# A hybrid delta-rule and gated-attention block: one table for the inverse norms, gate steps moved into the projections, turned v and k scaled on ScalarE

## The chip, the cores and the metric

The kernel runs on one core of one Trainium2 chip. The metric is the device time of one launch in microseconds; the median of three runs of the kernel before is given below. The engines are named as in the profile: PE (TensorE, matrix products; PEld its weight loads), DVE (VectorE), ACT (ScalarE), POOL (GpSimd), SP (SyncE, which issues the DMAs).

## The reference

The program computes two blocks over 512 tokens of width 1024. The second (three mixers with feed-forward layers) isn't touched by the change. The first is two hybrid layers, each:

```python
proj = x @ w_in                     # dn_q, dn_k, dn_v, dn_z, dn_b, dn_a, g_q, g_k, g_v, g_z, g_r
q, k, v = silu(causal_short_conv([dn_q, dn_k, dn_v], conv_w))     # 4 taps
q, k = l2norm(q) * 128 ** -0.5, l2norm(k)                         # 4 heads of 128
beta = sigmoid(dn_b)
g = -exp(a_log) * softplus(dn_a + dt_bias)
o_dn = head_rms_norm(gated_delta_rule_chunked(q, k, v, g, beta)) * silu(dn_z)
log_f = log_sigmoid(g_r @ gate_w2 + gate_b) / 16
o_gla = head_rms_norm(gla_chunked(g_q / 8, g_k, g_v, log_f)) * silu(g_z)
x = layer_norm(sqrt(2) * x + [o_dn, o_gla] @ w_out)
```

The delta rule works in chunks: with G the running sum of g within a chunk it needs exp(G_i - G_j) under a causal mask, v and k scaled by beta, k scaled by exp(G) and by exp(G_last - G), a triangular solve, and a scan over the chunks' states. The kernel takes chunks of 128 tokens.

## The kernel before, in words

All tiles hold features on the 128 partitions and the 512 tokens along the free axis, in float32; PSUM is eight banks of 128 x 512. A loop runs over the two layers. In each layer the phases follow one another, each a block in which every engine runs its own list of instructions, written out by hand, ordered against the others by semaphores alone; a phase begins when all engines have left the one before. SP clears the semaphores of the phase before at the start of the next.

**hybrid_projections (L321 to L726).** The input weights stream in 14 chunks of 128 x 2048. Each chunk is split into a high part (ACT, `high`, L226) and a low part (DVE, `low`, L237), as is the input (L220, L232), and each product is three matmuls (L251 to L253, or L271 to L273 where the tokens are on the output's partitions). `high(c)` waits for the tiles of chunk c-2 (the buffer is double), `low(c)` for `high(c)`, PE for `low(c)`. Chunks 0 and 1 (q and k of the gated attention) are interleaved by blocks: step n does block n of chunk 0 and block n - `behind` of chunk 1. Before them PE makes small sums (L428: gate rank and logits), which ACT copies (L534); after step 4 PE makes the gate logits from them (L447). ACT then has a chain on these (L539 to L546: bias, Abs, Exp, Ln), DVE goes on with it (L670 to L673: difference and running sum; `apart`, L647 and L648), and then splits chunk 2. ACT, after its chain, takes the first two tiles out, makes `high(2)`, takes the other two, copies `ba` (the beta and decay logits, turned by PE, L453), fills two slots, exponentiates twice (`falls`, L485), and makes `high(3)`. DVE's list for chunk 2 is `low(3)`, then `take(0)`, `take(1)`, ... (L637), which copy score pairs out of the banks. PE issues such a `pair` (L396) after every third block of chunks 2 to 7, and `pair(j)` waits for `take(j-2)`, since pairs use two pairs of banks in turn.

Chunks 8 to 13 are q, k, v of the delta rule: per tile a tap with the last weight on ACT (L505), three more taps on DVE (`conv`, L655), a Silu (L509), and for q and k a square (L515), a sum over the head by a matmul with ones (`sum_squares`, L407, banks 4 to 7 in turn), and the inverse norm `inverse` on ACT: Ln (L521) and then Exp (L524, L527); DVE multiplies it in (`normed`, L660). Inverses 0 to 3 stand in chunk 12's list, 4 to 7 in chunk 13's, two before each tap; `sum_squares(j)` waits for the Ln of `inverse(j-4)`. After chunk 13 come the Silus of the four v tiles.

**delta_gates (L729 to L874).** ACT loads a table that holds both Exp and Ln (`exp_and_log`, L120), and ACT and DVE alternate on tiles of 128 x 16 to make beta and g (L760 to L789). PE sums g (L848), DVE copies it out (L791, `gcol`). POOL spreads g and beta over matrices (L832), PE turns each into a row on all partitions by ones (L855); ACT makes exp of the G row (L771), DVE the differences (L797), `last` (L799), k beta (L801) and k beta exp(G) (L803), ACT the Exp of the differences (L773). POOL makes q exp(G) (L837), the chunk decay (L838) and the causal mask (L842). PE turns v and k (L863) in two banks in turn, and DVE scales them by a column of beta or of exp(G_last - G) as it takes them out (L813). Last, PE makes the products of k with k beta and with q (L872), and DVE multiplies the masked decay in (L821), which waits for all four masks.

**solve, scans, norms_and_output, layer_norm** follow and aren't touched.

Of the kernel before, what the change touches and what calls it, by code (L numbers as in the profile page):

```python
# [320 lines left out]
def hybrid_projections(nc, k, layer, h, gla):  # L321
# [9 lines left out]
    with operands(nc, k, KD), ExitStack() as stack, phase(  # L331
            nc, *GEMM, "parked", "tap", "conv", "silu", "small", "small_out", "logits", "small_turned", "act_step", "log_f",
            "sums", "filled", "slot_filled", "apart", "falls", "scaled", "pair", "taken", "end_arg", "end_exp", "k_end",
            "turned", "turned_read", "square", "square_sum", "inv_ln", "inv_norm", "normed", "z_silu",
            landed=k.landed) as s:
# [3 lines left out]
        small = stack.enter_context(sbuf(nc, "gate_rank_and_logits", [N_SMALL, T], F32))  # L339
        st = Stream(k, k.w_stream, layer * HYBRID_CHUNKS, PROJ_CHUNKS, CHUNK, 2, KD, x,  # L340
# [24 lines left out]
        with nc.Block() as block:  # L365
# [7 lines left out]
            def _(pe):  # L373
# [57 lines left out]
                behind = 2  # L431
                for step in range(KD + behind):
# [11 lines left out]
                    if step == 4:  # L444
# [37 lines left out]
            def _(act):  # L482
# [49 lines left out]
                st.input_high(act, s, 2, 5)  # L532
                act.wait_ge(s.small, 1)
# [24 lines left out]
                falls(1)  # L558
                st.high(act, s, 3, 1)
# [25 lines left out]
                for c in range(8, PROJ_CHUNKS):  # L585
# [33 lines left out]
            def _(dve):  # L619
# [57 lines left out]
                st.low(dve, s, 2, 0)  # L677
                for c in range(2, 8):
# [17 lines left out]
                for c in range(8, PROJ_CHUNKS):  # L696
# [10 lines left out]
                    conv(tile + 1)  # L707
                    if c == 12:
# [20 lines left out]
def delta_gates(nc, k, h, a):  # L729
# [5 lines left out]
    with ExitStack() as stack, phase(  # L735
            nc, "gate_act", "gate_dve", "g_ready", "gcol_sum",
            "gcol", "spread", "row", "row_exp", "diff", "row_read", "decay", "masked", "kb", "scaled", "turned", "turned_read",
# [3 lines left out]
        gt = sb("gate_steps", [P, 8, 16])  # L741
        beta = sb("beta", [P, TT, HEADS])
        g = sb("log_decay", [P, TT, HEADS])
        gcol = sb("g_column", [P, TT, HEADS])
# [5 lines left out]
        ba = h.ba[:].rearrange("p (t c) -> p t c", t=TT)  # L750

        def b16(n):
            return gt[:, n].rearrange("p (t h) -> p t h", t=TT)

        with nc.Block() as block:
            @block.scalar
            def _(act):
                exp_and_log(act)

# [1715 lines left out]
```

## Time and profile before

| | us |
|---|---|
| median of 3 runs (2411.50 to 2412.14) | 2411.68 |
| the profiled execution, its own time | 2410.51 |
| span of its trace | 2408.4 |
| mean granted clock of PE | 0.944 |
| one hybrid layer | 426.6 |

The profile is of one execution. The page gives busy time per engine over the whole span; a window gives it for a stretch, with the granted clock of PE (1.00 is 2.4 GHz, 0.50 is 1.2 GHz). A timeline row is start, duration, engine, line and operation; in brackets stands how long the engine had been idle and whose work ended that. Rows with x2 or more merge neighbours of one line. Durations of neighbours on one engine overlap a little, so start to start is less than their sum.

### The profile page before, as it was taken

Reading aid. Unit: us, or ns where it says so; the run is one execution under the profiler, and the core shown is the slowest. Engines: PE = TensorE matmul, PEld = TensorE weight load, DVE = VectorE, ACT = ScalarE, POOL = GpSimd, SP = SyncE. Lnnn points to the kernel's source line nnn. Section 1 sums busy time; section 2 is a strip of 40 time slices with the busy share of each in tenths; the row PEclk is TensorE's granted clock in tenths of the full one; section 3 lists DMA queues with packets and bytes.
Section 4 is the critical chain, followed back from the end, with each engine's and each line's share of the span. In section 5 each row is a group of like instructions: output and inputs, shape, how many; then the busy total and the mean of one; then the engine's idle time right before and its main releaser. Section 6 shows DMA issues by size and latency. Waiting matters only on the chain. (4 is left out here: it accounts for less than half of the span.)

```text
span 2408.4 us, 28383 instructions
## 1 busy us (share of the span) xinstructions
PE 2106.0 (87%) x11432; PEld 1626.7 (68%) x11432; DVE 1164.2 (48%) x1427; ACT 914.7 (38%) x1257; POOL 346.2 (14%) x332
## 2 busy tenths in 40 slices
PE   7996788799769959988889999979997868999996
PEld 4775586477548638734667788757886746778875
DVE  4444645444464551244367547533113756754753
ACT  4237333624732342255344224323222624432431
POOL 1200623020063300033210000020000022000002
PEclk9998799899979979999999999999999979999998
DMA  5111002221100212100112232212222001223221
GB/s 198 70 70 53 2 18 89 80 79 70 53 1 2 105 37 103 70 1 1 70 70 88 73 112 92 86 59 93 99 88 70 1 35 70 86 74 112 88 90 59
DMA packets 27158, 163.53 MB, mean 68 GB/s; under 512 B 2755, under 2 KB 6267, under 8 KB 11420
## 3 DMA queue, kind: packets, MB, share of 16 engines
q1 hardware_dynamic: 27036, 161.81, 18.9%
q8 instruction: 88, 1.44, 0.2%
q14 instruction: 34, 0.28, 0.0%
HBM read 155.47 MB, written 6.33 MB: 67 GB/s over the span
## 5 line engine op out<-in xcount | busy, mean ns | idle before, releaser
L251 PE MATMUL psum<-inputs_high,weights_high 128*128 128x512 f32 x928 | 376.5, 406 | 5.1 <-DVE inputs_low L232 5.1
L253 PE MATMUL psum<-inputs_high,weights_low 128*128 128x512 f32 x928 | 363.8, 392 | 0.0
L252 PE MATMUL psum<-inputs_low,weights_high 128*128 128x512 f32 x928 | 363.8, 392 | 0.0
L237 DVE TENSOR_TENSOR weights_low<-weights_raw,weights_high 128x2048 fp32r<-128x2048 f32 x72 | 169.4, 2353 | 324.7 <-ACT weights_high L226 324.7
L1771 PE MATMUL psum<-inputs_high,weights_high 128*128 128x512 f32 x704 | 278.8, 396 | 19.9 <-DVE weights_low L1763 11.1
L1772 PE MATMUL psum<-inputs_low,weights_high 128*128 128x512 f32 x704 | 275.7, 392 | 0.0
L1773 PE MATMUL psum<-inputs_high,weights_low 128*128 128x512 f32 x704 | 275.5, 391 | 0.0
L251 PEld LDWEIGHTS psum<-inputs_high,weights_high 128*128 128x128 f32 x928 | 175.6, 189 | 57.4 <-DVE inputs_low L232 7.9
L252 PEld LDWEIGHTS psum<-inputs_low,weights_high 128*128 128x128 f32 x928 | 175.6, 189 | 38.5 <-issue 3.8
L253 PEld LDWEIGHTS psum<-inputs_high,weights_low 128*128 128x128 f32 x928 | 175.5, 189 | 37.5
L1756 ACT CAST weights_high<-weights_raw 128x2048 fp32r<-128x2048 f32 (+1 forms) x76 | 126.7, 1669 | 178.1 <-PE psum L1773 174.8
L1771 PEld LDWEIGHTS psum<-inputs_high,weights_high 128*128 128x128 f32 x704 | 133.2, 189 | 56.1 <-DVE inputs_low L1903 16.4
L226 ACT CAST weights_high<-weights_raw 128x2048 fp32r<-128x2048 f32 x72 | 136.6, 1897 | 88.4 <-PE psum L253 37.5
L1763 DVE TENSOR_TENSOR weights_low<-weights_raw,weights_high 128x2048 fp32r<-128x2048 f32 (+1 forms) x76 | 152.5, 2006 | 36.1 <-ACT weights_high L1756 36.1
L1773 PEld LDWEIGHTS psum<-inputs_high,weights_low 128*128 128x128 f32 x704 | 133.2, 189 | 28.1
L1772 PEld LDWEIGHTS psum<-inputs_low,weights_high 128*128 128x128 f32 x704 | 133.3, 189 | 27.6 <-issue 0.5
L1771 PE MATMUL psum<-hidden_high,weights_high 128*128 128x512 f32 x352 | 140.2, 398 | 10.6 <-DVE weights_low L1763 10.1
L1929 DVE SCALAR_TENSOR_TENSOR conv<-up_scaled,second_parameters,conv 128x511 f32<-128x511 f32 (+1 forms) x176 | 131.9, 750 | 21.6 <-ACT conv L1859 18.5
L1772 PE MATMUL psum<-hidden_low,weights_high 128*128 128x512 f32 x352 | 139.7, 397 | 0.0
L1773 PE MATMUL psum<-hidden_high,weights_low 128*128 128x512 f32 x352 | 139.5, 396 | 0.0
L1922 DVE TENSOR_TENSOR up_scaled<-psum,inverse_rms 128x512 f32<-128x512 f32 x88 | 60.8, 691 | 109.9 <-PE psum L1773 105.8
L1859 ACT ACTIVATE conv<-up_scaled,second_parameters 128x512 f32<-128x512 f32 x88 | 71.9, 817 | 109.4 <-DVE up_scaled L1922 109.4
(317 smaller groups left out, 3360.8 us busy)
## 6 DMA issues: line engine op xcount, KB each, us to landing
weights_raw<-w_stream SPq DMA_DIRECT2D x116, 1024.0 KB, 4.8
weights_raw<-w_down SPq DMA_DIRECT2D x32, 704.0 KB, 4.1
residual_parked<-residual SPq DMA_DIRECT2D x2, 2048.0 KB, 11.1
residual_back<-residual_parked SPq DMA_DIRECT2D x2, 2048.0 KB, 7.9
residual<-x_t SPq DMA_DIRECT2D x1, 2048.0 KB, 7.9
out_t<-residual SPq DMA_DIRECT2D x8, 256.0 KB, 2.0
constants<-consts SPq DMA_DIRECT2D x1, 1537.5 KB, 11.7
table_backward<-bias_rows SPq DMA_DIRECT2D x1, 1024.0 KB, 5.5
```

Of the source, the lines that this page charges most:

```text
L226: act.copy(self.whi[:, u, 0:self.cols], self.raw[:, u, 0:self.cols]).then_inc(s.high, 1)
L237: dve.tensor_tensor(self.wlo[:, u, 0:self.cols], self.raw[:, u, 0:self.cols], self.whi[:, u, 0:self.cols].bitcast(F32), ALU.subtract).then ...
L251: pe.matmul(out, hi, self.ahi[:, k], start=start and b == 0, stop=False)
L252: pe.matmul(out, hi, self.alo[:, k], start=False, stop=False)
L253: mm = pe.matmul(out, lo, self.ahi[:, k], start=False, stop=stop and b == blocks - 1)
L1756: act.copy(whi[:, c % 2, 0:cols], raw[:, c % 2, 0:cols]).then_inc(s.high, 1)
L1763: dve.tensor_tensor(wlo[:, c % 2, 0:cols], raw[:, c % 2, 0:cols], whi[:, c % 2, 0:cols].bitcast(F32), ALU.subtract).then_inc(s.split, 1)
L1771: pe.matmul(out, wh, hi, start=start, stop=False)
L1772: pe.matmul(out, wh, lo, start=False, stop=False)
L1773: return pe.matmul(out, wl, hi, start=False, stop=stop)
L1859: act.activation(y[:, n % 2, yy], up[:, n % 2, yy], ACT.Identity, scale=taps[:, layer, 2, yy, n:n + 1], bias=bias[:, layer, yy, n:n + 1]). ...
L1929: dve.scalar_tensor_tensor(y[:, n % 2, yy, back:], up[:, n % 2, yy, 0:T - back], taps[:, layer, 2 - back, yy, n:n + 1], y[:, n % 2, yy, ba ...
```

## The change

The gate steps (L760 to L789) move from `delta_gates` into `hybrid_projections`: on ACT behind `falls(1)` and ahead of `high(3)`, on DVE behind `low(2)` and ahead of `low(3)`. The G sum (L848) moves to block 8 of chunk 9 on PE, its copy (L791) behind chunk 9's convolutions on DVE, and `sum_squares(0)` waits for it (the G sum lies in bank 6, which the sums of squares use in their turn). The table with Exp and Ln is loaded on ACT ahead of L534 and again ahead of `inverse(0)`. The gate logits L447 go from after step 4 to after step 0, and `behind` from 2 to 3. In `delta_gates` ACT in place of DVE scales the turned v and k, as four activations of 128 x 128 with a column as scale, placed between its Exps; PE's order mixes the turning with rows and products.

```diff
@@ hybrid_projections: phase gains gate_act, gate_dve, g_ready, gcol_sum, gcol; tile gate_steps [P, 8, 16]; b16, ba moved here
@@ tensor
                     elif j == 0:
                         pe.wait_ge(s.taken, n_pairs)
                         pe.wait_ge(s.turned_read, 2)
+                        pe.wait_ge(s.gcol, 1)
...
+                    elif c == 9 and b == 8:
+                        pe.wait_ge(s.g_ready, 1)
+                        pe.matmul(ps[:, 6, 0:16], con[:, K_INCL:K_INCL + P], h.g[:].rearrange("p t h -> p (t h)"),
+                                  start=True, stop=True).then_inc(s.gcol_sum, 1)
...
-                behind = 2
+                behind = 3
...
-                    if step == 4:
+                    if step == 0:
                         pe.wait_ge(s.small_out, 1)
@@ scalar
                 st.input_high(act, s, 2, 5)
+                exp_and_log(act)
                 act.wait_ge(s.small, 1)
...
                 falls(1)
+                act.wait_ge(s.small_out, 2)
+                act.activation(b16(0), ba[:, :, 0:HEADS], ACT.Exp, scale=-1.0).then_inc(s.gate_act, 1)
+                act.activation(gt[:, 7, 0:HEADS], par[:, C_ALOG:C_ALOG + HEADS], ACT.Exp).then_inc(s.gate_act, 1)
+                act.wait_ge(s.gate_dve, 1)
+                act.activation(b16(2), b16(1), ACT.Abs).then_inc(s.gate_act, 1)
+                act.wait_ge(s.gate_act, 3)
+                act.activation(b16(3), b16(2), ACT.Exp, scale=-1.0).then_inc(s.gate_act, 1)
+                act.wait_ge(s.gate_act, 4)
+                act.activation(b16(4), b16(3), ACT.Ln, bias=con[:, K_ONE:K_ONE + 1]).then_inc(s.gate_act, 1)
                 st.high(act, s, 3, 1)
...
                     elif c == 12:
+                        exp_and_log(act)
                         for j in range(4):
                             inverse(j)
@@ vector
                 st.low(dve, s, 2, 0)
+                dve.wait_ge(s.small_out, 2)
...
+                dve.tensor_tensor(b16(1), ba[:, :, HEADS:], dtb, ALU.add).then_inc(s.gate_dve, 1)
...
+                dve.scalar_tensor_tensor(h.g[:], b16(6), -1.0, rate, ALU.mult, ALU.mult).then_inc(s.g_ready, 1)
                 for c in range(2, 8):
...
                     conv(tile + 1)
+                    if c == 9:
+                        dve.wait_ge(s.gcol_sum, 1)
+                        dve.tensor_copy(h.gcol[:], ps[:, 6, 0:16].rearrange("p (t h) -> p t h", t=TT)).then_inc(s.gcol, 1)
@@ delta_gates: the gate steps, gcol and the waits for them go; beta, g, gcol come from h
@@ scalar
+                def turned(n):
+                    hd = n % HEADS
+                    act.wait_ge(s.turned, n + 1)
+                    for t in range(TT):
+                        col = beta[:, t, hd:hd + 1] if n < HEADS else last[:, 1, hd, t:t + 1]
+                        dst = a.vb if n < HEADS else a.kdec
+                        ins = act.activation(dst[:, t, hd], ps[:, 6 + n % 2, t * P:(t + 1) * P], ACT.Copy, scale=col)
+                    ins.then_inc(s.turned_read, 1)
                 exp_and_log(act)
...
                     act.activation(erow[:, n], ps[:, (2 * n) % 4], ACT.Exp).then_inc(s.row_exp, 1)
+                    if n >= 1:
+                        turned(n - 1)
                     act.wait_ge(s.diff, 4 * n + 4)
                     act.activation(decay[:, :, n], decay[:, :, n], ACT.Exp).then_inc(s.decay, 1)
                 act.wait_ge(s.last_arg, HEADS)
                 act.activation(last[:, 1], last[:, 0], ACT.Exp).then_inc(s.last_exp, 1)
+                turned(HEADS - 1)
+                act.wait_ge(s.last_exp, 1)
+                for n in range(HEADS, 2 * HEADS):
+                    turned(n)
@@ vector: the loop of eight multiplications (L805 to L814) goes
@@ tensor: row(n) and turn(n) are L851 to L856 and L859 to L865 as functions
+                for n in range(4):
+                    row(n)
+                turn(0)
+                turn(1)
+                for n in range(4, 2 * HEADS, 2):
+                    row(n)
+                    row(n + 1)
+                    turn(n // 2)
+                for n in range(HEADS, HEADS + 2):
+                    turn(n)
                 pe.wait_ge(s.kb, HEADS)
                 for n in range(2 * TT):
...
                     mm.then_inc(s.pair, 1)
+                    if n in (1, 3):
+                        turn(HEADS + 2 + n // 2)
```

## Rows read from the trace of the kernel before

**Rows 1.** The page of the profiled execution: span, and busy time of TensorE.
```profile
span 2408.4 us, 28383 instructions
...
PE 2106.0 (87%) x11432; PEld 1626.7 (68%) x11432; DVE 1164.2 (48%) x1427; ACT 914.7 (38%) x1257; POOL 346.2 (14%) x332
```

**Rows 2.** One line's instructions: the last gate step, once in each layer.
```profile
L789 DVE SCALAR_TENSOR_TENSOR log_decay<-gate_steps x2: 174/174/174, 246.6 to 673.2; 128x16 f32<-128x16 f32 x2
```

**Rows 3.** Windows of layer 0: length; busy us (instructions) PE, PEld, DVE, ACT, POOL; PEclk, DMA, GB/s.
```profile
24.40:49.10 24.70, 24.63 (x105) 18.85 (x104) 8.12 (x11) 11.93 (x15) 0.00 (x0) 1.00 0.29 120
...
52.10:57.70 5.60, 5.59 (x18) 4.04 (x19) 1.21 (x1) 4.34 (x4) 3.90 (x3) 0.50 0.49 187
...
276.40:328.00 51.60, 44.25 (x1138) 42.24 (x1139) 26.34 (x56) 15.64 (x26) 31.52 (x24) 0.90 0.01 3
```

**Rows 4.** Timeline, start of layer 0: start, us, engine, line, op [idle <-releaser].
```profile
24.60 0.58 ACT L534 COPY gate_rank_and_logits<-psum 40x512 f32<-40x512 f32 x1 [2.42 <-PE psum L428]
...
37.69 1.26 ACT L539 ACTIVATE k_end<-psum,layer_parameters 128x512 f32<-128x512 f32 x2 [10.94 <-PE psum L447]
...
45.14 1.90 ACT L226 CAST weights_high<-weights_raw 128x2048 fp32r<-128x2048 f32 x1
...
52.11 0.79 PE L271 MATMUL psum<-weights_high,inputs_high 128*128 128x512 f32 x1 [3.07 <-DVE weights_low L237]
...
54.57 1.88 ACT L226 CAST weights_high<-weights_raw 128x2048 fp32r<-128x2048 f32 x1
...
58.84 0.76 DVE L637 COPY_PREDICATED gla_scores<-constants,psum 128x512 f32<-128x512 int32 x1
...
62.73 0.49 PE L396 MATMUL psum<-gla_qk 64*128 64x128 f32 x4
```

**Rows 5.** Last projection chunk of layer 0: one group of lines, then the timeline.
```profile
L521 ACT ACT_TABLE_LOAD x8 | 10.3, 1283 | 0.1
...
208.53 0.69 ACT L521 ACTIVATE inverse_norm<-psum,constants 128x512 f32<-128x512 f32 x1
...
212.56 0.69 ACT L521 ACTIVATE inverse_norm<-psum,constants 128x512 f32<-128x512 f32 x1
...
221.47 1.10 PE L407 MATMUL psum<-squares,constants 128*128 128x512 f32 x2 [0.87 <-ACT inverse_norm L521]
...
224.25 0.40 PE L253 MATMUL psum<-inputs_high,weights_low 128*128 128x512 f32 x1
...
239.60 0.67 ACT L505 ACTIVATE conv<-psum,layer_parameters 128x512 f32<-128x512 f32 x1
...
241.59 2.19 ACT L509 ACTIVATE qkv<-conv 128x512 f32<-128x512 f32 x4
```

**Rows 6.** Timeline of the delta gates of layer 0.
```profile
244.05 1.28 ACT L120 ACT_TABLE_LOAD   x1 [0.27 <-PEq L365]
...
246.04 0.31 ACT L767 ACTIVATE gate_steps<-gate_steps,constants 128x16 f32<-128x16 f32 x1
...
246.82 0.61 PE L848 MATMUL psum<-log_decay,constants 128*128 128x16 f32 x2 [22.17 <-DVE log_decay L789]
246.91 1.05 POOL L832 TENSOR_TENSOR spread<-constants,log_decay 128x512 f32<-128x512 f32 x1 [120.62 <-DVE log_decay L789]
...
266.25 0.64 POOL L842 TENSOR_SCALAR_AFFINE_SELECT decay<-decay 128x512 f32<-128x512 f32 x1
...
268.98 0.69 DVE L821 TENSOR_TENSOR a_transposed<-psum,decay 128x512 f32<-128x512 f32 x1 [0.20 <-PE psum L872]
...
275.70 0.69 DVE L821 TENSOR_TENSOR attention<-psum,decay 128x512 f32<-128x512 f32 x1 [0.20 <-PE psum L872]
```

**Rows 7.** Timeline: TensorE's first product of the solve, layer 0.
```profile
278.11 0.68 PE L933 MATMUL psum<-constants,coupling 64*64 64x64 f32 x16 [2.46 <-POOL coupling L1010]
```

**Rows 8.** Groups of lines by form: the turned copies, and a 128x128 activation.
```profile
L813 DVE TENSOR_TENSOR v_beta<-psum,beta 128x512 f32<-128x512 f32 x4 | 2.7, 684 | 0.8 <-PE psum L863 0.8
...
L2183 ACT ACTIVATE scores<-scores,negative_maxima 128x128 f32<-128x128 f32 x72 | 27.8, 388 | 30.8 <-DVE negative_maxima L2159 30.8
```

More of the change, by code:

```diff
@@ L339, in hybrid_projections, with b16 @@
         small = stack.enter_context(sbuf(nc, "gate_rank_and_logits", [N_SMALL, T], F32))
+        gt = stack.enter_context(sbuf(nc, "gate_steps", [P, 8, 16], F32))
+        ba = h.ba[:].rearrange("p (t c) -> p t c", t=TT)
+        def b16(n):
+            return gt[:, n].rearrange("p (t h) -> p t h", t=TT)
         st = Stream(k, k.w_stream, layer * HYBRID_CHUNKS, PROJ_CHUNKS, CHUNK, 2, KD, x,
@@ L735, in delta_gates @@
     with ExitStack() as stack, phase(
-            nc, "gate_act", "gate_dve", "g_ready", "gcol_sum",
-            "gcol", "spread", "row", "row_exp", "diff", "row_read", "decay", "masked", "kb", "scaled", "turned", "turned_read",
+            nc, "spread", "row", "row_exp", "diff", "row_read", "decay", "masked", "kb", "scaled", "turned", "turned_read",
             "last_arg", "last_exp", "pair", "pair_read") as s:
@@ L740, in sb @@
             return stack.enter_context(sbuf(nc, name, shape, F32))
[L741 to L744, printed above, removed]
+        beta, g, gcol = h.beta, h.g, h.gcol
         spread = sb("spread", [P, 2, TT, P])
@@ L757, in _ @@
             def _(act):
-                exp_and_log(act)
-                act.activation(b16(0), ba[:, :, 0:HEADS], ACT.Exp, scale=-1.0).then_inc(s.gate_act, 1)
-                act.activation(gt[:, 7, 0:HEADS], par[:, C_ALOG:C_ALOG + HEADS], ACT.Exp).then_inc(s.gate_act, 1)
-                act.wait_ge(s.gate_dve, 1)
-                act.activation(b16(2), b16(1), ACT.Abs).then_inc(s.gate_act, 1)
-                act.wait_ge(s.gate_act, 3)
-                act.activation(b16(3), b16(2), ACT.Exp, scale=-1.0).then_inc(s.gate_act, 1)
-                act.wait_ge(s.gate_act, 4)
-                act.activation(b16(4), b16(3), ACT.Ln, bias=con[:, K_ONE:K_ONE + 1]).then_inc(s.gate_act, 1)
+                def turned(n):
[6 more added lines that the diff above has]
+                    ins.then_inc(s.turned_read, 1)
+                exp_and_log(act)
                 for n in range(HEADS):
@@ L803, in _ @@
                     dve.tensor_tensor(a.kbg[:, n], kb[:, n], erow[:, n], ALU.mult).then_inc(s.scaled, 1)
-                for n in range(2 * HEADS):
-                    hd = n % HEADS
-                    dve.wait_ge(s.turned, n + 1)
-                    if n == HEADS:
-                        dve.wait_ge(s.last_exp, 1)
-                    src = ps[:, 6 + n % 2].rearrange("p (t e) -> p t e", t=TT)
-                    col = beta[:, :, hd] if n < HEADS else last[:, 1, hd]
-                    dst = a.vb if n < HEADS else a.kdec
-                    dve.tensor_tensor(dst[:, :, hd], src, col.unsqueeze(2).to_broadcast([P, TT, P]),
-                                      ALU.mult).then_inc(s.turned_read, 1)
                 for n in range(2 * TT):
@@ L846, in _, with row @@
             def _(pe):
-                pe.wait_ge(s.g_ready, 1)
-                pe.matmul(ps[:, 6, 0:16], incl, g[:].rearrange("p t h -> p (t h)"), start=True, stop=True) \
-                    .then_inc(s.gcol_sum, 1)
-                for n in range(2 * HEADS):
+                def row(n):
                     pe.wait_ge(s.spread, n + 1)
@@ L856, in _, with turn @@
                               start=True, stop=True).then_inc(s.row, 1)
-                pe.wait_ge(s.gcol, 1)
-                for n in range(2 * HEADS):
+                def turn(n):
                     src = v if n < HEADS else kk
```

35 lines of the change are left out of this document (13 added, 22 removed).

## The prediction

> **What bounds the kernel now.** I read the page first: TensorE (PE) is busy 87% of a span of 2408.4 us [rows 1]. That is an average, so I read the windows of layer 0 next, with the granted clock beside them, then the timeline around the holes. Everything that the change touches lies in the two hybrid layers; the same steps stand 426.6 us later in layer 1 [rows 2], so each term below is worked out for layer 0 and taken twice.
>
> Three holes matter. **The start:** PE is full from 24.4 to 49.1, then stands still for 3.07 us until VectorE (DVE) has split chunk 2, and works on at half clock (1.2 GHz) until about 57.7 [rows 3, 4]. DVE was late because its chain (log of the gate, scan, `apart`) hangs on ScalarE's L539, which waited 10.94 us for PE's logits and began at 37.69 only. **The end of the projections:** PE ends its last product at 224.65, but ScalarE (ACT) works on until 243.78, on eight inverse norms of which each is two table loads of 1.28 us around an Ln and an Exp [rows 5]. PE itself waits there too, for a bank that a late Ln frees (the row shows 0.87; there are three of 0.84 to 0.87). **The delta gates:** from 244.05, GpSimd (POOL) can't begin until 246.91, because the small gate steps come first; its work then runs to 266.89, DVE's products with the mask run from 268.98 to 276.39 [rows 6].
>
> **Part 1, the start.** The preload of the common table (1.28) falls where ACT waits 2.42 us for L428's sums [rows 4]: free. The logits are issued after step 0 instead of step 4. Two steps of 6 and three of 12 products come before them now, so 42 products come off their front; at 24.63 us for some 100 products [rows 3] that is about 10 us. ACT's chain then ends near 33 and DVE is through with `apart` near 39, so the split of chunk 2 hangs on its high half alone, which began at 45.14 and ended at 47.04. With `behind` 3 chunk 0 has 6 fewer products of chunk 1 before its end, 1.4 us: high half at 45.7. From the end of a high half to the end of its split the rows show 2.4 (56.45 to 58.84) [rows 4]: ready at 48.1, before PE ends chunk 1 at 49.0. So the stall of 3.07 and the half clock behind it (5.6 us at half speed, 2.8 lost) go.
>
> What is late next: `pair(2)`, which may not start before DVE's `take(0)`, queued behind the split of chunk 3. ACT loses the load before its Exps (1.28) and gets the gate steps, whose five activations took 245.33 to 246.35, 1.0 us with their handovers [rows 6]. L226 thus starts at 54.3 for 54.57, `take(0)` ends near 59.35, and `pair(2)` starts at 59.4. PE would be there at 62.73 - 3.07 - 2.8 = 56.9, so it waits 2.5. **Gain: 62.73 - 59.4 = 3.3 us.** Queued behind ACT's new waits is only that high half; DVE's new steps fill its wait for it. Bounds: 5.9 if the new wait doesn't exist; 0 if the clock falls again behind it and costs as much as the one that goes. Here the trace warns: behind a hole of 2.46 us (PE at 278.11) the stage ran at 0.90 of the clock [rows 3, 7]. I take 3.3: PE is full on both sides of the new hole, while the thin gate stage lay before the one of 2.46. The Trainium skill (TensorE: Matmul & The Clock Gate, "Why this matters for your kernels") sets its limit at gaps of more than some 3 us. By it the clock stays and 3.3 stands; by the row of the 2.46 us hole it may fall and this part be worth 0. The range keeps both.
>
> **Part 2, chunk 9.** The G matmul (L848, 0.61 us at half clock for its two passes [rows 6]) now stands in a stretch where PE is full: **cost 0.3**. Its copy is done by DVE after two convolutions and holds up `sum_squares(0)` if late; it is small and due in chunk 10, so I count nothing; if that cover were gone it costs under 1 us.
>
> **Part 3, one table.** The 16 loads per layer (8 of them stand in the L521 group, 8 at L524 and L527) become one preload. Ln to Ln was 212.56 - 208.53 = 4.03; less two loads it is 1.46 [rows 5]. That loads aren't put back is shown by the gate steps: Exp, Exp, Abs, Exp, Ln behind one L120 load, none between [rows 6]. ACT needs 1.28 + 8 x 1.46 + a tap of 0.7 from 207.2, so 220.9 if never waiting; the last inverse waits for its sum of squares, at 221.47 - 2.6 + 1.1 = 220.0, and ends at 221.5. PE loses its waits, 2.57, and ends at 222.1: it is the later, so PE sets the end. Behind it the chain is the one of before: tap(11) at 239.60 to the end of the last Silu at 243.78, 4.18 us (it hides the Silu load, the convolution runs beside). New end 222.1 + 4.2 = 226.3. **Gain 17.5 us.** Bounds: 15 if PE keeps its waits, 18 if the Silus overlap better.
>
> **Part 4, the delta gates.** POOL starts at once: 246.91 - 244.1 = 2.8 us. Its twelve steps per head took 19.98 us to the end of the last mask at 266.89 [rows 6] and are untouched, but the row matmuls now have transposes between them: I put 0.6 on it. DVE loses its eight multiplications (0.69 each, 5.5 us [rows 8]) that stood between its head loop and its products, so it no longer comes 22.07 us after POOL's start (268.98) but waits for the mask: 20.6. The eight products took 7.4; with the last two transposes of k among PE's products I give them 7.8. Sum 28.4 for 29.48: 1.1 us. **Gain 3.9 us.** This needs ACT to keep up. Its new operation, 128x128 with a column scale, isn't in the trace; the nearest row is the 128x128 Exp with a column bias, 388 ns [rows 8], so 32 are 12.4 us at most, and with eight Exps of 0.6 to 0.7 that is below 18 in a stage where 20.6 pass before DVE needs anything: hidden, though each head's mask Exp may now come up to 1.5 us later, which POOL's queue covers. Bounds: 0 (the interleaving and a slow clock eat all) and 6 (clock at full, spreads no longer waiting for half-speed rows). No DMA is added, and SP's clears of five semaphores only change phase.
>
> **Sum.** 3.3 - 0.3 + 17.5 + 3.9 = 24.4 a layer, 48.8 for both. The profiled execution took 2410.51 (span 2408.4): 2361.7. The median of the runs is 1.2 higher: **2362.9 us**.
>
> **Rivals.** *A, the delta stage gives nothing (still faster).* If ACT's scaled copies or the shuffled PE queue make masks late, part 4 is 0: 41 us gained, 2371. For it: each head now has one more ACT step in its loop of about 2.6 us. Chance 0.12. *B, the loads come back.* If the compiler reloads per function after a preload of another phase, 16 loads stay and one joins (1.3), and the gate steps add two loads ahead of chunk 3's high half, 2.6 us more wait at `pair(2)`: part 1 is about -2.5 with the clock down, part 3 -1.3, part 4 +3.9: 0, 2412. Against it: the Ln at L767 had none [rows 6]. Chance 0.03. *C, slower: ACT becomes the bound of the delta stage.* The 32 copies run in PE's and DVE's way: PE may not turn the next tile before ACT has read the last but one. ACT is covered up to 20.6 us with about 5 taken, so up to 0.49 us a copy; beyond, each 0.1 us costs 3.2 a layer. To undo the 24.4 takes 32x = 15.6 + 24.4, x = 1.25 us; at 1.4 us the run is 2 x 4.8 slower, 2421. The nearest row is 0.388. Chance 0.02. The Trainium skill (ScalarE: Activation LUTs, "Rules for kernel authors") speaks for C in kind: multiplications belong on VectorE, ScalarE being slower at them. The trace agrees as to size (0.69 for 512 columns on DVE against four of up to 0.39 on ACT), yet DVE was in the way and ACT idle for most of the stage, so the row of the path, not of the engine, decides.
>
> **How the numbers follow.** The forecast has 0.83, A 0.12, B 0.03, C 0.02. Slowest end of the range: part 1 at 0, part 3 at 15.5, part 4 at 0: 15.2 a layer, 2381. Fastest: 5.9, 18 and 5.5: 29 a layer, 2353. Only B and C and a little else lie outside. A measurement of this kernel tells 0.2% (4.8 us) from no change. Faster 0.95, same 0.03, slower 0.02.
>
> **What would show it.** Part 1: chunk 2 starts at 49.1 with no wait, a wait of about 2.5 for `gla_scores` stands before the third pair, and the granted clock says whether it was dear. Part 3: no load between 209 and 223, PE without waits in chunk 13, ACT's last Silu at about 4.2 after PE's end. Part 4: POOL's first spread within 0.4 us of the phase's start, DVE idle ahead of its first product until POOL's last mask, eight groups of four copies of under 0.4 us on ACT. The prediction is wrong if the tail behind PE's last product is longer than 6 us, or if chunk 2 still waits for its split.

## The result, and the profile after

The changed kernel takes 2370.91 us (median of 4 runs, 2369.7 to 2372.03) against 2411.59 of the kernel before, run beside it: a ratio of 0.9834 (95% interval 0.9817 to 0.9851). That is 40.7 us gained where 48.8 were forecast; it lies inside the range. Its profiled execution took 2370.67.

The page of the kernel after, as [rows 1] before:

```profile
span 2368.9 us, 28397 instructions
...
PE 2104.9 (89%) x11432; PEld 1630.0 (69%) x11432; DVE 1157.6 (49%) x1411; ACT 888.5 (38%) x1289; POOL 343.4 (14%) x332
```

PE is as long busy as before (2106.0) and waits some 38 us less. Of the stages, measured in each trace between the same events (in us, layer 0 and layer 1):

| stage, from and to | before | after | gained, both | forecast |
|---|---|---|---|---|
| start: first small product to the last pair's end | 132.49, 132.70 | 132.69, 131.35 | 1.15 | 6.6 |
| on to tap 9 (holds the G matmul) | 59.12, 59.12 | 59.32, 59.36 | -0.4 | -0.6 |
| tail: tap 9 to the last Silu's end | 37.25, 37.25 | 19.06, 19.06 | 36.4 | 35.0 |
| delta gates: to the last product with the mask | 32.62, 32.72 | 28.59, 28.24 | 8.5 | 7.8 |
| solve, scans, norms, out product | 137.88, 137.97 | 139.52, 139.51 | -3.2 | 0 |
| layer norm | 22.14, 22.07 | 22.88, 24.44 | -3.1 | 0 |
| loop back: its end to layer 1's first product | 4.91 | 6.77 | -1.9 | 0 |
| second block and end | 1545.32 | 1543.37 | 1.95 | 0 |

These and 0.2 ahead of the first product make the 39.6 us between the spans. Parts 2 to 4 came within 1.4 us of their forecasts. Two things did not come as forecast: the start, and stages whose code is the same. Each column is one trace, and one code varies from trace to trace: the start of both layers is 265.2 us here before and 263.2 in e1 below, which has the same code there, and 263.1 to 264.8 in five traces with the changed start (after, e2, e5, e8, e10). So the 1.15 us of the start aren't clear of that spread; the 36.4 and the 8.5 are.

**The start** of the kernel after, timeline of layer 0, against [rows 4]: first PE, then POOL, then DVE, each engine's rows by themselves.

```profile
47.82 0.50 PE L271 MATMUL psum<-weights_high,inputs_high 128*128 128x512 f32 x1
...
60.11 1.22 PE L402 MATMUL psum<-gla_qk 64*128 64x128 f32 x8 [4.05 <-DVE gla_scores L659]
...
51.25 1.52 POOL L758 TENSOR_TENSOR qkv<-gla_qk,qkv 128x512 f32<-128x512 f32 x1 [50.73 <-ACT qkv L496]
52.73 1.51 POOL L760 TENSOR_TENSOR qkv<-gla_qk,qkv 128x512 f32<-128x512 f32 x1
54.20 1.53 POOL L758 TENSOR_TENSOR qkv<-gla_qk,qkv 128x512 f32<-128x512 f32 x1
55.70 1.49 POOL L760 TENSOR_TENSOR qkv<-gla_qk,qkv 128x512 f32<-128x512 f32 x1
...
52.26 0.55 DVE L704 TENSOR_SCALAR gate_steps<-gate_steps 128x16 f32<-128x16 f32 x1 [3.79 <-ACT gate_steps L572]
52.84 0.25 DVE L706 RECIPROCAL beta<-gate_steps 128x16 f32<-128x16 f32 x1
53.05 1.23 DVE L708 SCALAR_TENSOR_TENSOR gate_steps<-gate_steps 128x16 f32<-128x16 f32 x1
54.31 1.46 DVE L711 SCALAR_TENSOR_TENSOR log_decay<-gate_steps 128x16 f32<-128x16 f32 x1
55.70 3.64 DVE L237 TENSOR_TENSOR weights_low<-weights_raw,weights_high 128x2048 fp32r<-128x2048 f32 x1
59.26 1.31 DVE L659 COPY_PREDICATED gla_scores<-constants,psum 128x512 f32<-128x512 int32 x2
```

Chunk 2 starts without a wait, at 47.82. But the third pair waits 4.05 us. The last gate step took 0.174 us in the delta stage [rows 2] and takes 1.46 here. Look at the ends: L704 at 52.81, L708 at 54.28, L711 at 55.77, each within 0.05 us of the end of one of POOL's products (52.77, 54.24, 55.73); and the split L237, 3.64 us long, is what is left of POOL's fourth product (to 57.19) plus 2.15, about its usual 2.29. The reciprocal isn't held up. The number of operands doesn't explain that, since L704, which like it reads one tile (and a constant), is held up. In layer 1 the four gate rows have the same lengths, but the split goes ahead of POOL's fourth product instead of behind it, by 0.01 us, and the wait is 2.77:

```profile
464.94 2.28 DVE L237 TENSOR_TENSOR weights_low<-weights_raw,weights_high 128x2048 fp32r<-128x2048 f32 x1
...
464.95 3.63 POOL L760 TENSOR_TENSOR qkv<-gla_qk,qkv 128x512 f32<-128x512 f32 x1
```

The windows around layer 0's wait, with [rows 3] as their counterpart:

```profile
47.80:56.00 8.20, 8.20 (x45) 5.88 (x43) 3.85 (x6) 6.94 (x12) 4.75 (x4) 1.00 0.33 128
56.00:60.10 4.10, 0.07 (x1) 0.02 (x1) 4.10 (x3) 0.00 (x0) 1.19 (x1) 0.88 0.00 0
60.10:65.90 5.80, 5.79 (x21) 4.25 (x23) 1.20 (x2) 0.00 (x0) 0.00 (x0) 0.50 0.50 181
```

PE was full up to the hole and came back at 1.2 GHz for about 5.8 us, which costs 2.9. In layer 1 the half clock behind the wait of 2.77 lasts 3.4 us and costs 1.7. The length isn't fixed by the hole: behind the same hole of 3.07 us PE ran at half clock for 5.6 and 5.8 us in the two layers of the kernel before and for 3.4 in e1's layer 0, whose start is 2.2 us shorter, 1.1 of it by this.

**The tail**, timeline of ACT, against [rows 5]:

```profile
207.42 1.28 ACT L120 ACT_TABLE_LOAD   x1
208.71 0.69 ACT L532 ACTIVATE inverse_norm<-psum,constants 128x512 f32<-128x512 f32 x1
209.43 0.72 ACT L535 ACTIVATE inverse_norm<-inverse_norm,constants 128x512 f32<-128x512 f32 x1
210.06 0.67 ACT L532 ACTIVATE inverse_norm<-psum,constants 128x512 f32<-128x512 f32 x1
...
220.23 0.63 ACT L538 ACTIVATE inverse_norm<-inverse_norm 128x512 f32<-128x512 f32 x1
221.59 0.69 ACT L516 ACTIVATE conv<-psum,layer_parameters 128x512 f32<-128x512 f32 x1 [0.73 <-PE psum L253]
222.29 1.28 ACT L520 ACT_TABLE_LOAD   x1
223.59 2.19 ACT L520 ACTIVATE qkv<-conv 128x512 f32<-128x512 f32 x4
```

One load stands ahead of eight inverses, Ln to Ln is 1.35 where it was 4.03, and the last Silu ends 4.2 us after PE's last product.

**The delta gates**, timeline, against [rows 6]: POOL's first and last row, DVE's products, ACT's and PE's rows on the turned tiles.

```profile
226.06 1.05 POOL L840 TENSOR_TENSOR spread<-constants,log_decay 128x512 f32<-128x512 f32 x1 [99.78 <-POOLq L371]
...
245.95 0.62 POOL L850 TENSOR_SCALAR_AFFINE_SELECT decay<-decay 128x512 f32<-128x512 f32 x1
...
246.68 1.29 DVE L831 TENSOR_TENSOR a_transposed<-psum,decay 128x512 f32<-128x512 f32 x2 [4.64 <-POOL decay L850]
...
234.30 1.14 ACT L794 ACTIVATE v_beta<-psum,beta 128x128 f32<-128x128 f32 x4 [1.02 <-PE psum L868]
...
242.24 2.18 ACT L794 ACTIVATE k_decayed<-psum,to_last 128x128 f32<-128x128 f32 x8
...
242.41 0.66 PE L868 MATMUL psum<-constants,qkv 128*128 128x128 f32 x4 [1.92 <-ACT v_beta L794]
```

POOL starts 0.29 us after the Silus; DVE now idles 4.64 us until POOL's last mask. A group of four scaled copies takes 1.14 us.

### The profile page after: what moved, and what is told of

It is laid out like the page before. It is cut to its first block and busy times, and to the rows that moved or that the text cites. A ratio compares the mean times of both kernels' runs of the same rounds, so it can differ in the third digit from the quotient of the medians.

```text
span 2368.9 us, 28397 instructions
## 1 busy us (share of the span) xinstructions
PE 2104.9 (89%) x11432; PEld 1630.0 (69%) x11432; DVE 1157.6 (49%) x1411; ACT 888.5 (38%) x1289; POOL 343.4 (14%) x332
## 5 line engine op out<-in xcount | busy, mean ns | idle before, releaser
L237 DVE TENSOR_TENSOR weights_low<-weights_raw,weights_high 128x2048 fp32r<-128x2048 f32 x72 | 170.4, 2366 | 328.4 <-ACT weights_high L226 328.4
L1789 PE MATMUL psum<-hidden_high,weights_high 128*128 128x512 f32 x352 | 140.4, 399 | 10.6 <-DVE weights_low L1781 10.2
```

The lines of the kernel that those rows point to most:

```text
L237: dve.tensor_tensor(self.wlo[:, u, 0:self.cols], self.raw[:, u, 0:self.cols], self.whi[:, u, 0:self.cols].bitcast(F32), ALU.subtract).then ...
L1789: pe.matmul(out, wh, hi, start=start, stop=False)
```

## The experiments

Twelve kernels ran in three lots of four, each lot on one chip beside the kernel before; ratios are compared, since the lots' medians of before differ (2413.6, 2414.71, 2413.27). "After" in an edit means the changed kernel.

| kernel | us | ratio, 95% interval |
|---|---|---|
| e1_table_only | 2380.22 | 0.9860, 0.9844 to 0.9877 |
| e2_no_table | 2407.92 | 0.9980, 0.9970 to 0.9989 |
| e3_high_first | 2363.79 | 0.9794, 0.9777 to 0.9810 |
| e4_gates_behind | 2363.53 | 0.9800, 0.9783 to 0.9817 |
| e5_dve_turned | 2373.00 | 0.9833, 0.9814 to 0.9852 |
| e6_gates_home | 2367.04 | 0.9815, 0.9789 to 0.9841 |
| e7_pool_waits | 2364.76 | 0.9806, 0.9782 to 0.9831 |
| e8_after_again | 2373.28 | 0.9838, 0.9816 to 0.9860 |
| e9_both | 2361.16 | 0.9787, 0.9772 to 0.9802 |
| e10_longer_code | 2371.67 | 0.9833, 0.9820 to 0.9846 |
| e11_home_high_first | 2367.33 | 0.9815, 0.9802 to 0.9828 |
| e12_high_first_again | 2360.70 | 0.9780, 0.9765 to 0.9795 |

### The table alone, and all but the table

e1 is the kernel before with one line; e2 is after without it:

```diff
                     elif c == 12:
+                        exp_and_log(act)
                         for j in range(4):
                             inverse(j)
```

> The kernel before, with one line added: the common table is loaded ahead of the first inverse norm; nothing else of the change. Theory (the tail of the projections is nearly all of the gain): the stretch from the last tap of chunk 12 to the last Silu shrinks by 18.2 us a layer, as in the changed kernel, so about 36 us in all, 2375 for 2411.6. Rival (the tail owes part of its gain to the gate steps or the sum of g having left the next phase, or the untouched stages give some of it back whatever the change): 30 us or less. No load between the Lns and Exps of chunk 12 and 13 in either case.

> The changed kernel without its preload ahead of the first inverse norm; everything else stays. Theory: 16 loads come back in each layer and the run takes about 36 us more than the changed one, 2407, so that all the other parts together are worth some 4 to 5 us against the kernel before. Rival (the parts need one another): 2395 or less, or more than 2412.

e1 gained 33.4 us and e2 5.7 by their medians. In e1's trace the tail is 19.02 us in both layers for 37.25: the line is worth 18.2 a layer, 36.5 in all. By the medians 3 us of it were given back where nothing had changed, so e1 lies between its theory (about 36) and its rival (30 or less). In e2, which came out as expected (2407.92 for 2407), the 16 loads a layer stand as before: 8 of each layer at the Ln, in this group, which counts both layers, and as many at the two Exps.

```profile
L532 ACT ACT_TABLE_LOAD x16 | 20.5, 1283 | 0.3
```

So by the tails that one line is 36.4 of the 40.7 us. Parts 1, 2 and 4 together, forecast at 13.8 us, brought 5.7 (e2) to 7.3 (2411.59 less 2370.91 less 33.4).

### Where the start's gain went

Four edits of after. In e3 ACT splits chunk 3 ahead of its slot copies, falls and gate steps, and DVE does its gate steps behind the take of the second pair; in e4 the slot copies and falls stay first:

```diff
+                st.high(act, s, 3, 1)
                 act.wait_ge(s.freed, TT)
                 for slot in range(2):
...
-                st.high(act, s, 3, 1)
                 falls(2)
```

and in both, on DVE (the twelve lines of the gate steps are taken from behind the split of chunk 2):

```diff
                         take(j)
+                        if j == 1:
+                            dve.wait_ge(s.small_out, 2)
...
+                            dve.scalar_tensor_tensor(h.g[:], b16(6), -1.0, rate, ALU.mult, ALU.mult).then_inc(s.g_ready, 1)
```

> The changed kernel with the high half of chunk 3 ahead of the two slot copies, the falls and the gate steps on ScalarE, and VectorE's gate steps behind take(1). Theory (chunk 2's third pair waits because chunk 3's split is late, and this split and the small gate steps are stretched by GpSimd's scaling beside them): the split ends before GpSimd begins, near 52.5 in layer 0, the third pair waits for nothing, and PE's clock stays full; 7.4 us less in layer 0 (4.05 of waiting and 3.4 of half clock) and 4.5 in layer 1, 2359. Rival (the wait only moves on to a later pair, or GpSimd's later start is the next to be late): less than 4 us gained, 2367 or more.

> The changed kernel with the gate steps behind the high half of chunk 3 on ScalarE and behind take(1) on VectorE; the slot copies and falls stay ahead of it. Theory (VectorE's gate steps took 3.4 us in place of 0.8 beside GpSimd, and held up chunk 3's split): the split begins as soon as the high half ends, near 53.9 in layer 0 for 55.7, still beside GpSimd's scaling; the third pair waits some 2 us for 4.05, and the clock may or may not fall; 2 to 8 us gained in all. Rival (the order of the gate steps doesn't matter, the split alone is what GpSimd stretches): within 2 us of the changed kernel. VectorE's two small scalar_tensor_tensor steps take under 0.3 us each where GpSimd is idle and over 1 us where it multiplies.

In e6 the gate steps, the G matmul and its copy are back in the delta stage, as in the kernel before:

```diff
                 falls(1)
-                act.wait_ge(s.small_out, 2)
-                act.activation(b16(0), ba[:, :, 0:HEADS], ACT.Exp, scale=-1.0).then_inc(s.gate_act, 1)
...
                 st.high(act, s, 3, 1)
```

e7 is after with one wait more, so that POOL stands still during the gate steps:

```diff
+                pool.wait_ge(s.g_ready, 1)
                 for n in range(n_levels):
                     scale(n)
```

> The changed kernel with the gate steps of the delta rule back in their own stage (the matmul and copy of the running sum too); the earlier logits, the later pairs (three chunks behind), both tables and ScalarE's scaling stay. My theory is that the gate steps, stretched beside POOL's scaling, are what made the wait at the third pair 4.05 us: without them the low halves of chunk 3 begin as the high halves end, and the wait is 1 to 2.5 us. The delta stage then pays 2.85 us a layer again until POOL's first spread (3.14 for 0.29). The start should give back 1.5 to 3 a layer of it, so the time is 2371 plus or minus 3. The rival is that the wait comes of the order (pairs three chunks behind need the takes earlier) and not of the gate steps: then it stays at 3 to 4 us and the time is 2376 to 2378.

> The changed kernel in which POOL begins its scaling of q and k only when the last gate step is done. Nothing is left out. My theory is that VectorE's short steps on 16 columns are stretched by POOL's products beside them (0.55, 1.23 and 1.46 us where the same steps took 0.17 to 0.18 in the delta stage before). With POOL idle they should take 0.17 to 0.25 each and the five be done within 1.6 us of the first of ScalarE's (3.7 now), and the low halves of chunk 3 should begin as the high halves end, 0.9 us earlier than now, so the wait at the third pair falls by 0.9 us or more, to about 3 or less, if POOL's later start holds nobody up. The rival is that the steps are slow by their waits on ScalarE or by their place: then their own durations stay at 0.5 to 1.5 us. In the time either is small: 2366 to 2374.

e7's timeline, layer 0, DVE then POOL then PE:

```profile
52.71 0.18 DVE L704 TENSOR_SCALAR gate_steps<-gate_steps 128x16 f32<-128x16 f32 x1 [3.78 <-ACT gate_steps L572]
52.92 0.25 DVE L706 RECIPROCAL beta<-gate_steps 128x16 f32<-128x16 f32 x1
53.50 0.17 DVE L708 SCALAR_TENSOR_TENSOR gate_steps<-gate_steps 128x16 f32<-128x16 f32 x1 [0.33 <-ACT gate_steps L579]
53.70 0.18 DVE L711 SCALAR_TENSOR_TENSOR log_decay<-gate_steps 128x16 f32<-128x16 f32 x1
55.29 2.35 DVE L237 TENSOR_TENSOR weights_low<-weights_raw,weights_high 128x2048 fp32r<-128x2048 f32 x1 [1.41 <-ACT weights_high L226]
...
53.96 1.53 POOL L758 TENSOR_TENSOR qkv<-gla_qk,qkv 128x512 f32<-128x512 f32 x1 [53.45 <-DVE log_decay L711]
55.45 3.56 POOL L760 TENSOR_TENSOR qkv<-gla_qk,qkv 128x512 f32<-128x512 f32 x1
...
58.45 0.72 PE L402 MATMUL psum<-gla_qk 64*128 64x128 f32 x8 [1.93 <-DVE gla_scores L659]
```

This settles the mechanism. The same instructions, with the same waits on ACT, take 0.17 to 0.18 us with POOL idle for 0.55, 1.23 and 1.46, and the wait falls from 4.05 to 1.93. And it works both ways: here the split started ahead of POOL's second product (55.29 for 55.45), keeps its 2.35 us, and it is that product that takes 3.56. In these rows whoever starts first goes through and the other waits to its end. The Trainium skill states this (SBUF — State Buffer, "SBUF: two separate sides"): an operation of VectorE in a mode that uses two ports, or one with two inputs in SBUF against a GpSimd operation that reads SBUF, and the GpSimd operation exclude each other for a whole instruction. The trace agrees, with the numbers above; by that rule the stretch could have been forecast, and the prediction didn't weigh it. In which mode L704 and the reciprocal ran, no run shows.

The wait and what it costs, in all versions with pairs three chunks behind (both layers; "start" is the first row of the table above):

| kernel | wait at the third pair | clock behind it | start |
|---|---|---|---|
| after again (e8) | 4.05, 2.77 | half | 132.53, 130.68 |
| e7, POOL idle | 1.93, 1.99 | half, for less long | 130.03, 129.61 |
| e6, gates home | 1.14, 1.21 | full | 127.13, 128.10 |
| e4, gates behind | 1.14, 1.21 | full | 128.44, 127.62 |
| e12, chunk 3 first | none | full | 127.72, 126.18 |

The windows of e12, the same stretch as above, and its gate steps:

```profile
50.00:57.00 7.00, 7.00 (x41) 5.06 (x39) 4.91 (x5) 6.01 (x10) 2.79 (x2) 1.00 0.62 229
57.00:66.00 9.00, 9.00 (x55) 6.43 (x53) 6.37 (x9) 0.32 (x1) 3.18 (x3) 1.00 0.10 43
```

```profile
55.76 1.51 DVE L710 TENSOR_SCALAR gate_steps<-gate_steps 128x16 f32<-128x16 f32 x1
57.30 0.25 DVE L712 RECIPROCAL beta<-gate_steps 128x16 f32<-128x16 f32 x1
57.47 1.27 DVE L714 SCALAR_TENSOR_TENSOR gate_steps<-gate_steps 128x16 f32<-128x16 f32 x1
58.77 1.45 DVE L717 SCALAR_TENSOR_TENSOR log_decay<-gate_steps 128x16 f32<-128x16 f32 x1
```

The steps are as stretched there as in after (1.51, 1.27, 1.45), and PE has no wait: it isn't the collision but its place ahead of the split of chunk 3 that cost time. e4 shows the same with the slot copies and falls left first: its wait is e6's, 1.14 and 1.21, though the gate steps stay. With both repaired, e12's start is 4.8 and 4.5 us shorter than e8's.

Against what was expected: e3 had its clean start, but took 2363.8 for the 2359 of its theory (the rival said 2367 or more); its starts are 9.6 us shorter than after's, for 11.9 expected, and its delta stages 2.5 longer, with the code there unchanged. e4 was expected to wait some 2 us and to gain 2 to 8; it waited 1.14 and gained 7.4 by the medians. e3 and e4 can't be told apart by their times. e6's wait and its delta stages (2.8 us a layer more) came as expected, its median is 1 us below the expected range.

e7's expected limit of 3 us for the wait held; its median is lower than expected (8.5 below e8 with 3.6 in the starts), and their intervals overlap, so I rest nothing on the rest.

### What the move of the gate steps is worth

e11 is e6 with chunk 3 split first; e12 is e3 once more.

```diff
+                st.high(act, s, 3, 1)
                 act.wait_ge(s.freed, TT)
...
                 falls(1)
-                st.high(act, s, 3, 1)
```

> The changed kernel with the gate steps back in the delta stage, and ScalarE splitting chunk 3 ahead of its slot copies and falls. With the start free of its wait in either version, this prices the move of the gate steps by itself: POOL's first spread 2.85 us a layer later than with the steps moved, so 5.7 us above the version that splits chunk 3 first with the steps moved, about 2368 to 2370. The rival is that the moved steps cost the start as much as they spare the delta stage: then it is within 2 us of that version, at 2362 to 2366.

> The version that splits chunk 3 first, with the gate steps behind the take of the second pair, once more on the chip of these runs, as the measure for the other three: 2362 to 2366 and a ratio of 0.979 to 0.981 if its first result holds. The rival, that its lead of 7 us over the changed kernel was the chip's, would put the ratio at 0.982 or more.

Beside a clean start, moving the steps is worth 6.6 us by the medians (2367.33 less 2360.70), near the 5.7 expected, and the two intervals don't overlap; e12's ratio, a little below its expected 0.979, repeats e3's. The stages show less: the delta stages of e11 are 62.3 together for 58.4 in e12, 3.9 us, while e12's starts are 0.8 longer and its stretches to tap 9 0.5. Where the other 4 us of the medians lie isn't shown. As the change places them, the steps earned nothing: e6, with them at home, is 6.2 us below e8 by its median (their intervals overlap). Its starts are 8.0 us shorter together and its delta stages 5.7 longer.

### ScalarE's scaling, and the loop back

e5 gives the turned tiles back to DVE in the old order; e10 is e5 with as many instructions as the scaling had, which do nothing for the result and for which nobody waits; e8 is after itself; e9 is e12 with e5's edit. First e5's, of which only the core is shown, then e10's:

```diff
-                    if n >= 1:
-                        turned(n - 1)
...
+                for n in range(2 * HEADS):
...
+                    dve.tensor_tensor(dst[:, :, hd], src, col.unsqueeze(2).to_broadcast([P, TT, P]),
+                                      ALU.mult).then_inc(s.turned_read, 1)
```

```diff
                 act.activation(last[:, 1], last[:, 0], ACT.Exp).then_inc(s.last_exp, 1)
+                for n in range(32):
+                    act.copy(spare[:, n:n + 1], con[:, K_ONE:K_ONE + 1])
```

> The changed kernel with one part of the change undone: VectorE, not ScalarE, scales the eight turned v and k tiles, one 128x512 product each, in the old order (all eight rows, then all eight turns, then the pairs). My theory is that this part is worth little, because POOL's masks, which end 20.5 us after its first spread, set when the decay products may begin, and VectorE idles 4.64 us ahead of them. The eight products at 0.68 us are 5.5 us, so the last decay product should come 9.5 us after the last mask (as before) in place of 7.8: 1.7 us a layer, 3.4 in all, so 2374 us and a ratio near 0.984 where the changed kernel has 0.983. The rival is that ScalarE's four short copies a tile (1.14 us) hold its exponentials up as much as they spare VectorE: then the masks would end earlier here (by over 1 us) and the time would be the same or better (2371 or under). If the longer loop back to layer 1 (6.16 us from the last scaled tile to the parameters' copy, for 3.27 before) comes of the 32 more ScalarE instructions, it should be near 3.3 again.

> The changed kernel once more, on the chip of these runs, for a second look at the stages that it doesn't touch. If the 4 us a layer that they gave back belong to the kernel, the loop back to layer 1 takes 5.5 us or more again and the half-clock phases of the inverse, the scans and the last stages fall as before, and the ratio is 0.982 to 0.985. The rival is that they differ from run to run: then some of these lengths come out otherwise by over 1 us, with the same time within 2 us.

> The changed kernel with VectorE scaling the turned v and k (the loop back to layer 1 took 3.27 us there), and with 32 small ScalarE copies of one column added behind its last exponential of the delta stage, where ScalarE waits for nothing that follows. They are as many instructions as ScalarE's scaling had. If the longer loop back comes of the length of ScalarE's code between the layer's start and its end, it takes 5.6 to 6.5 us again from the last scaled tile to the parameters' copy, and the time rises by about 1.9 us to 2373 to 2375. The rival is that it comes of what ScalarE's scaling does (its reads of PSUM, the order of TensorE's turns): then it stays at 3.3 us and the time at that of the kernel without the copies, 2371 to 2373.

> Both earlier repairs together: ScalarE splits chunk 3 ahead of its slot copies, falls and gate steps, VectorE's gate steps stand behind the take of the second pair, and VectorE scales the turned v and k in the old order of the delta stage. My theory, from the runs so far: ScalarE's scaling gives about 1.0 us in the two delta stages and costs about 1.9 us in the loop back to layer 1 (5.06 us there without it, 6.90 with it), so this is faster than the version that only splits chunk 3 first by about 1 us, and lies between 2361 and 2364. The rival is that the half-clock stretches of TensorE in the delta stage and behind it decide: then it is level with that version or up to 2 us slower.

The delta stages take 28.24 and 29.94 us in e5 for 28.60 and 28.57 in e8: the scaling earns 1.0 us in both together (e5's expected 1.7 a layer came in layer 1 only), and 1.7 between e9 and e12 (60.06 and 58.35). That is little beside the spread: e3 and e12, one kernel, differ by 0.9 there, and e10, with e5's code but for the idle copies, takes 60.05. Then look at ACT in the loop back, its first row in layer 1, of after, of e5 and of e10:

```profile
421.11 1.28 ACT L1383 ACT_TABLE_LOAD   x1 [4.35 <-issue]
```

```profile
418.77 1.28 ACT L1371 ACT_TABLE_LOAD   x1 [1.45 <-PEq L151]
```

```profile
418.15 1.28 ACT L1374 ACT_TABLE_LOAD   x1 [4.54 <-issue]
```

In after ACT waits 4.35 us for nothing that the profile shows; in e5 that is gone, and 32 idle copies bring it back. So it is the length of ACT's code that costs, not its work. The page's queue table goes with it: this queue of instructions has 34 packets in before, e1, e5 and e9, 39 in all the others, and exactly those others have the long loop back (6.2 to 7.1 us from the end of the layer norm to the next first product; 4.9 to 5.4 in the four). Of before and of after:

```profile
q14 instruction: 34, 0.28, 0.0%
```

```profile
q14 instruction: 39, 0.32, 0.0%
```

The Trainium skill (Runtime: NRT & Kernel Launch, "Instruction fetch mechanics") says that instructions are fetched ahead in sequence and that a taken branch to a block not at hand waits for its fetch; the traces fit that, with 1.8 us here (6.90 less 5.06), but show no fetch. That the packets belong to ACT is inferred from these kernels alone. Loss and gain cancel: e5 and e8 have ratios 0.9833 and 0.9838, and e9, expected 1 us faster than e12, is level with it at 0.9787 and 0.9780: its loop back is 1.9 us shorter and its delta stages 1.7 longer. e10's total was expected 1.9 us above e5 and is not; its ratio is the same, 0.9833. An effect of that size is seen in the stages only, not in the medians.

### The stages that gave back

e8 came at the ratio expected (0.9838) and repeats after's long loop back (6.90 for 6.77) and its layer norm of layer 1 (24.39 for 24.44). But over all fourteen traces (before, after and the twelve) the same code takes 22.1 to 24.6 us in the layer norm and 137.2 to 140.4 from the solve to the out product, and the two runs of one kernel, e3 and e12, differ in both layer norms (24.56 and 22.89 for 22.90 and 22.11). In the layer norm what differs is the clock. The stretch behind the out product in layer 1, windows of before and of after, columns as in [rows 3]:

```profile
841.06:856.66 15.60, 9.70 (x19) 3.88 (x18) 5.59 (x10) 6.89 (x11) 1.26 (x1) 0.89 0.00 0
```

```profile
801.05:819.02 17.97, 12.07 (x19) 4.55 (x18) 5.59 (x9) 6.90 (x11) 1.26 (x1) 0.72 0.00 0
```

The same 19 products are busy 2.4 us longer at a mean clock of 0.72 for 0.89, and that is the whole difference. This stage is thin, that is, PE idles for 12.4 us of it in either trace, and runs partly at half clock; which of its products fall into the half-clock stretches differs from trace to trace.

The 3.2 us from the solve to the out product aren't all clock. In layer 1 PE is busy 1.4 us longer there. In layer 0 it is busy as long as before (123.6 for 123.9) at the same mean clock (0.94), and waits 1.9 us more. The waits for the low half of the inputs (L232) grew, of before and of after, in us, times, longest:

```profile
PE psum L251 <- DVE inputs_low L232: 1.1, 2, 0.6
```

```profile
PE psum L251 <- DVE inputs_low L232: 3.4, 4, 1.5
```

Why a given run gets its half clock and these waits where it does stays open; I ran nothing that moves a stage in time without changing it.

## Why the prediction was right, and where it was not

**Right in sign and in range, 8 us off in the time, and nearly all of that has two causes.** Against the forecast of 48.8 the traces show: start 1.2 for 6.6 (with 0.2 more ahead of it), part 2 -0.4 for -0.6, part 3 36.4 for 35.0, part 4 8.5 for 7.8, untouched stages -6.2 for 0.

**Part 1 failed in two steps.** The stall of 3.07 us did go. The step that cost most is "I take 3.3: PE is full on both sides of the new hole", which kept the clock up. It fell, at a cost of 2.9 us in layer 0 and 1.7 in layer 1. The sum said 3.3; layer 0 gave -0.2 and layer 1 1.35, so the clock is nearly all of the miss. The lower bound of 0 had foreseen it. It would have fallen behind the forecast wait of 2.5 us too, as far as the rows tell: behind a wait of 2.71 in e10's layer 0 and of 1.93 in e7's the clock was at half for 3.4 us.

The other step is "DVE's new steps fill its wait for it". The price of the steps was taken from a place where POOL stood idle, and the prediction noted no engine beside them. ACT's high half began at 52.92, earlier than the 54.3 put down, and PE came at 56.07 for 56.9. With the 2.3 us of an undisturbed split, and a take behind it, the pair could have gone near 58; the steps and the stretched split made it 60.11, for 59.4 forecast, a wait of 4.05 for 2.5.

The warning that the prediction took from [rows 3, 7], a hole of 2.46 us, was the better guide than the limit of 3 us that the Trainium skill gives (TensorE: Matmul & The Clock Gate, "Why this matters for your kernels"). The traces disagree with that limit: waits of 1.93, 1.99 and 2.77 us with PE full on both sides were all followed by half clock, and waits of 1.14 and 1.21 were not.

**Part 3** was right by its own steps: one load, Ln to Ln 1.35 for the 1.46 put down, the last inverse at 220.9 for 221.5, PE's last product at 221.55 for 222.1, 4.2 behind it. **Part 4** too: first spread 0.29 for "within 0.4", masks 20.5 for 20.6, products 7.8 for 7.8. Its copies took 1.14 us for four, below the 1.55 of the row at 388 ns. Rival C is refuted with it, and B by the loads. Rival A named 2371, and the time is 2371; yet its mechanism is wrong, as the delta stage gave 8.5 us. A right number was no proof of a cause.

**The untouched stages** had no term at all. 1.9 us of their 6.2 are traced to the change: the loop back, which 32 more instructions on ACT made longer. The layer norms' 3.1 are clock, which differs between two runs of one kernel by as much as 1.7 us a stage. The solve to the out product's 3.2 are clock in part and longer waits of PE in part; neither is shown to come of the change.

**A faster version came of it.** Chunk 3 split first and the gate steps behind the second take: 0.9780 (0.9765 to 0.9795) on one chip and 0.9794 on another, 10 to 14 us below the changed kernel by their ratios to before (0.9834 and 0.9838 for that).

## What to carry to other kernels

Price a small VectorE step by what GpSimd does where it will stand, not where it stood: beside GpSimd's products it lasts until the product ends (of the steps here all but the reciprocal), and if a split or take is queued behind it, TensorE pays. Put such steps behind the instruction that TensorE waits for, and they cost under 1 us a layer. Price the half clock behind a new wait of TensorE as well as the wait: at the start of these layers each of 1.93 us or more was followed by it, at 1.7 to 3.1 us. And when a tail hangs on table loads, make the one-line edit first and by itself: here e1 had 33.4 of the 40.7 us.

## What the runs showed of the hardware that was not expected

- Short steps of VectorE (scalar_tensor_tensor on two tiles, tensor_scalar on one) took 0.17 to 0.18 us alone and 0.55 to 1.51 beside POOL's products of 1.5 us; a reciprocal of the same size kept its 0.25. POOL's product in turn took 3.56 us beside a split that had started first.
- 32 more ScalarE instructions in the looped layer cost 1.8 to 2.0 us at the loop back, in a wait that has no releaser in the profile, and five more packets on an instruction queue.
- TensorE fell to 1.2 GHz behind a single hole of 1.93 us in a stretch that was otherwise full, and did not behind 1.14 and 1.21. Behind one and the same hole of 3.07 us it ran there for 5.6 to 5.9 us in three cases and for 3.4 in a fourth.
- Copies of 128x128 from PSUM with a column scale on ScalarE took 1.14 us for four and 2.18 for eight, 0.26 for each further one; the bound had been 0.388.
